# A 4-layer-style hybrid decoder step: the intra-chunk matrix of its gated recurrence built from blocks of four quarters instead of by halving

## The chip, the core and the metric

The kernel runs on one core of one Trainium2 chip. A core has five engines with instruction streams of their own, which meet only at semaphores: TensorE (PE in the profile, its weight loads PEld), VectorE (DVE), ScalarE (ACT), GpSimd (POOL) and SyncE (SP), which here issues the DMAs. SBUF holds working data in 128 partitions, PSUM takes the results of matmuls. The metric is the device time of one execution in microseconds (us), lower is better.

## The reference, cut to what matters

Two layers. Each projects its input, runs sliding-window attention on one part of the columns and a gated linear recurrence (HGRN2) on the other, multiplies both by gates, and maps them to the output. The prompt has 2048 tokens, and 8 samples of 8 tokens each are decoded beside it. The part at issue is the recurrence, four heads of 128 by 128:

```python
G = jnp.cumsum(gc, axis=1)                 # running sum of log forget gates
diff = G[:, :, None] - G[:, None, :]
decay = jnp.exp(jnp.where(causal, diff, NEG_INF))
A = jnp.einsum('bthd,bshd,btshd->bhts', qc, kc, decay)
o = einsum('bhts,bshv->bthv', A, vc) + einsum('bthd,bhdv->bthv', qc * exp(G), S)
S = exp(G_last)[..., None] * S + einsum('bshd,bshv->bhdv', kc * exp(G_last[:, None] - G), vc)
```

A[t, s] is the sum over the 128 key dimensions d of q[t,d] k[s,d] exp(G[t,d] - G[s,d]), for s up to t. The exponent is at most 0. Factors exp(G[t]) and exp(-G[s]) can't be applied apart over a long stretch, since exp(-G[s]) grows without bound, so a kernel picks a token m between s and t and uses exp(G[t]-G[m]) and exp(G[m]-G[s]), both at most 1.

## The kernel before

The kernel is written by hand in phases, each with one instruction stream per engine: constants, and then for each of the two layers attention, recurrence and output. All engines meet at a barrier between phases. The order on an engine is the order in the code, nothing schedules it. Waits are on named semaphores. `wait_apart` puts a wait on a semaphore increment of its own ahead of the instruction.

The recurrence phase walks 17 tiles of 128 tokens, tile 0 being the 64 sample tokens. All tensors of a tile hold heads and tokens in the free dimension (4 x 128 = 512 columns) and key dimensions in the partitions. Its functions are `front` (DVE), `front_log` and `front_exp` (ACT), which turn the projections of a tile into `kT` and the running sum `G`; `middle` on each engine, which builds A; and `output_and_update` on PE. `front` of tile n+1 stands behind `middle` of tile n on DVE.

A is built by seven levels, of half-block lengths 64, 32, 16, 8, 4, 2, 1. A level of length h covers, in each block of 2h tokens, the pairs with t in the second half and s in the first:

- DVE, `sub_level` (L1181, L1182): two subtractions of 256 columns each write the exponents of both halves to E.
- ACT, `middle` (L1046): one exponential of 512 columns on E.
- POOL, `level` (L960): two products, q times E (256 columns, compact in qE) and k times E (256 columns, in kE).
- PE, `level` (L1353): for each of four heads a matmul of kE (128 x 128 weights) with 64 columns of qE, into the PSUM bank LV.
- DVE, `take_level` (L1193): one predicated copy of 256 columns takes from LV what belongs to the level's blocks, with the mask `levels`.

E, qE, kE and LV have two buffers each, used in turn. Last come four matmuls of q and k without decay (`diagonal`, L1360) into the bank M and a copy of the diagonal (L1226, 512 columns). A matmul of float32 data counts as two MATMUL instructions in the trace (8 instructions for the four heads of a level), one of the projections (split into rounded parts, float32r) as one.

PE interleaves this with the projections of the next tile, in `step` (from L1393): q(n+1), levels 0 and 1, transposes of the finished tile's result (L1343), f(n+1), levels 2 and 3, transposes of q and f (L1335, L1337, which need ACT's copy `zqf`, L1011), half of g(n+1), level 4, the other half of g, levels 5 and 6, the diagonal, v(n+1), the transposes of k (L1367), output and state update (L1376 to L1382). Tile 1 and the last tile have levels with no projection between them.

## Time and profile before

| | us |
|---|---|
| median of 3 runs (3099.20 to 3102.58) | 3102.14 |
| profiled execution, its own time | 3102.25 |
| its span, first to last instruction | 3100.6 |
| PE busy | 2827.0 (91%) |
| DVE busy | 1585.9 (51%) |
| POOL busy | 1058.6 (34%) |
| ACT busy | 1026.2 (33%) |

The span runs from the first to the last instruction, and the execution takes 1.65 us more. The shares are means over three kinds of phase. In layer 0 attention ends at about 387 us, the recurrence runs until about 1045 us, and the output phase until about 1540 us; layer 1 follows in the same shape. In a row of a timeline the first number is the start, the second the duration, and in brackets stands how long the engine had been idle and what released it. The duration of an instruction reaches about 0.1 us into the next one where two follow each other freely, so the cost of one in a row of many is the distance between starts. A row with "x8" merges eight instructions that follow one another.

### The profile page before, as it was taken

How to read it: one execution, taken by the hardware profiler on the slowest of the kernel's cores; microseconds unless marked ns; L12 is line 12 of the kernel's file. 1: busy time of each engine (PE TensorE's matmuls, PEld its weight loads, DVE VectorE, ACT ScalarE, POOL GpSimd, SP SyncE). 2: the span in 40 equal slices, each digit the busy share in tenths (PEclk: the TensorE clock that was granted, in tenths of full speed). 3: DMA queues.
4: the chain of work that ended last, by engine and by line, in shares of the span. 5: the costliest groups of instructions: out<-in, count | busy, mean ns of one | idle time of the engine just before them, and what ended most of it. 6: DMA issues, size and time to landing. Idle time of an engine off the chain costs nothing. (4 is left out here: it accounts for less than half of the span.)

```text
span 3100.6 us, 43735 instructions
## 1 busy us (share of the span) xinstructions
PE 2827.0 (91%) x15322; PEld 2373.2 (77%) x15322; DVE 1585.9 (51%) x3037; ACT 1026.2 (33%) x2172; POOL 1058.6 (34%) x940
## 2 busy tenths in 40 slices
PE   6999869999999489999869998699999995899998
PEld 5777658888888478888657776588888884788886
DVE  4666655666766532222246666556666665322222
ACT  3333233444444411111133332334444444111111
POOL 1222122555555323333112221225555553233331
PEclk9999978999999699999889998789999996999999
DMA  4111311000000412222231113110000004122221
GB/s 152 41 41 41 124 38 58 25 21 27 20 24 14 177 58 87 86 86 86 93 111 41 41 41 124 38 58 25 21 27 20 24 14 177 58 87 86 86 81 61
DMA packets 96923, 195.20 MB, mean 63 GB/s; under 512 B 10913, under 2 KB 56225, under 8 KB 94753
## 3 DMA queue, kind: packets, MB, share of 16 engines
q1 hardware_dynamic: 96832, 194.05, 18.6%
q8 instruction: 50, 0.82, 0.1%
q14 instruction: 41, 0.33, 0.0%
HBM read 135.10 MB, written 60.82 MB: 63 GB/s over the span
## 5 line engine op out<-in xcount | busy, mean ns | idle before, releaser
L103 PE MATMUL r_Z<-w_rec_high,w_rec_xh 128*128 128x512 f32 x1088 | 446.4, 410 | 39.2 <-POOL w_rec_xl L951 30.7
L103 PE MATMUL r_Z<-w_rec_high,w_rec_xl 128*128 128x512 f32 x1088 | 430.5, 396 | 0.0
L103 PE MATMUL r_Z<-w_rec_low,w_rec_xh 128*128 128x512 f32 x1088 | 429.6, 395 | 0.0
L103 PE MATMUL a_Z<-w_attn_high,w_attn_xh 128*128 128x512 f32 (+1 forms) x816 | 303.2, 372 | 0.0
L103 PE MATMUL a_Z<-w_attn_low,w_attn_xh 128*128 128x512 f32 (+1 forms) x816 | 291.8, 358 | 0.0
L103 PE MATMUL a_Z<-w_attn_high,w_attn_xl 128*128 128x512 f32 (+1 forms) x816 | 291.0, 357 | 0.0
L1353 PEld LDWEIGHTS r_LV<-r_qE,r_kE 128*128 128x128 f32 x1840 | 249.1, 207 | 51.8 <-POOL r_kE L960 31.0
L960 POOL TENSOR_TENSOR r_qE<-r_qT,r_E 128x256 f32<-128x256 f32 x230 | 191.1, 831 | 281.2 <-ACT r_E L1046 152.3
L1353 PE MATMUL r_LV<-r_qE,r_kE 128*128 128x64 f32 x1840 | 250.4, 290 | 34.9 <-POOL r_kE L960 25.3
L103 PEld LDWEIGHTS r_Z<-w_rec_high,w_rec_xh 128*128 128x128 f32 x1088 | 209.0, 192 | 79.2 <-issue 40.7
L1193 DVE COPY_PREDICATED r_A<-levels,r_LV 128x256 f32<-128x256 int32 x230 | 121.6, 529 | 250.6 <-issue 166.9
L1758 PE MATMUL o_MX<-w_out_high,o_mh 128*128 128x512 f32 x512 | 204.1, 399 | 45.4 <-DVE w_out_low L140 45.4
L103 PEld LDWEIGHTS r_Z<-w_rec_high,w_rec_xl 128*128 128x128 f32 x1088 | 207.7, 191 | 46.5
L103 PEld LDWEIGHTS r_Z<-w_rec_low,w_rec_xh 128*128 128x128 f32 x1088 | 209.2, 192 | 39.3
L1046 ACT ACTIVATE r_E<-r_E 128x512 f32<-128x512 f32 x230 | 145.3, 633 | 265.8 <-DVE r_E L1182 265.8
L1587 POOL TENSOR_TENSOR o_ml<-o_mraw,o_mh 128x1024 fp32r<-128x1024 f32 x34 | 83.6, 2458 | 405.6 <-ACT o_mh L1638 405.6
L1758 PE MATMUL o_GT<-w_out_high,o_hh 128*128 128x512 f32 x544 | 216.1, 397 | 0.0
L960 POOL TENSOR_TENSOR r_kE<-r_kT,r_E 128x256 f32<-128x256 f32 x230 | 213.0, 926 | 0.0
L1758 PE MATMUL o_GT<-w_out_high,o_hl 128*128 128x512 f32 x544 | 212.9, 391 | 0.0
L1758 PE MATMUL o_GT<-w_out_low,o_hh 128*128 128x512 f32 x544 | 212.8, 391 | 0.0
L1758 PE MATMUL o_MX<-w_out_high,o_ml 128*128 128x512 f32 x512 | 201.3, 393 | 0.0
L1758 PE MATMUL o_MX<-w_out_low,o_mh 128*128 128x512 f32 x512 | 200.7, 392 | 0.0
(247 smaller groups left out, 5622.1 us busy)
## 6 DMA issues: line engine op xcount, KB each, us to landing
w_attn_xraw<-dram_xT SPq DMA_DIRECT2D x34, 512.0 KB, 3.4
r_xraw<-dram_xT SPq DMA_DIRECT2D x34, 512.0 KB, 3.3
o_mraw<-dram_mixT SPq DMA_DIRECT2D x34, 512.0 KB, 4.4
dram_y_all<-o_hb SPq DMA_DIRECT2D x34, 512.0 KB, 2.9
dram_xT<-o_yT SPq DMA_DIRECT2D x34, 512.0 KB, 5.2
w_rec_whole<-dram_w_in SPq DMA_DIRECT2D x16, 1024.0 KB, 12.1
w_attn_whole<-dram_w_in SPq DMA_DIRECT2D x16, 640.0 KB, 8.1
dram_mixT<-a_mixT SPq DMA_DIRECT2D x136, 64.0 KB, 2.1
```

The source lines that it names most:

```text
L103: mm = pe.matmul(out, a[:, c, :], b[:, c, :], start=(first and c == chunks[0] and a is xh and b is wh), stop=(last and c == chunks[-1] and ...
L960: op = pool.tensor_tensor(to, halves(flat(q_or_k), h)[half], halves(E[i][:, :], h)[half], ALU.mult)
L1046: act.activation(E[l % 2][:, :], E[l % 2][:, :], ACT.Exp).then_inc(S["level_exp"], 1)
L1193: dve.copy_predicated(to, mask, src).then_inc(S["level_took"], 1)
L1353: mm = pe.matmul(LV[i][:, 64 * g:64 * g + 64], kE[i][:, g * P:(g + 1) * P], qE[i][:, g, :], start=True, stop=True)
L1587: pool.tensor_tensor(ml[:, :, :], mraw[:, :, :], mh[:, :, :].bitcast(F32), ALU.subtract)\
L1758: mm = pe.matmul(out[0][:, out[1]], a[:, c, :], w, start=(c == 0 and a is high and b is wh), stop=(c == chunks - 1 and a is low))
```

## The change

A is now built in three rounds of four-quarter blocks, quarter lengths m = 32, 8, 2, each cut in two units of two heads (`units`, six in a tile), and then one step of neighbouring tokens together with the diagonal.

In a block of 4m tokens with quarters 0 to 3, all six pairs of a later with an earlier quarter are covered at once. The key side has three scaled quarters (each to its own end, 192 columns for two heads, kE). The query side has six slots: quarters 1, 2, 3 scaled from the end of the quarter before them, quarters 2, 3 from two before, and quarter 3 from three before (`LAGS`; 192, 128 and 64 columns for two heads). Per unit:

- DVE, `spans`: four subtractions (192, 192, 128, 64 columns) in place of two of 256.
- ACT: one exponential of 576 columns in place of 512.
- POOL, `scale`: four products (192, 192, 128, 64 columns) in place of two of 256.
- PE, `unit`: two matmuls of 192 columns in place of four of 64.
- DVE, `take`: three predicated copies (192, 128, 64 columns), each behind a wait for the one before, in place of one of 256.

Behind the six units `spans_next` (DVE, 256 columns), an exponential of 256 columns and `scale_next` (POOL, 256 columns) prepare the odd tokens for their left neighbours. `q_next` holds q's 128 tokens and those 64 side by side, so four matmuls of 192 columns (`neighbours`), two into each LV bank, give both the diagonal and the neighbours. `take_next` copies them in four dependent copies (128 and 256 columns, for each pair of heads). The diagonal no longer uses the bank M. Tile 0 takes two units (m = 2) in place of three levels.

The masks of the quarters are made on DVE in the constants phase, from the table that was loaded before, by 19 small instructions, each waited for. DMAs are the same. The sample states' row products now lie in E instead of kE.

On DVE, the end of `middle` in a tile of the loop, with the buffer numbers; r_LV0 and r_LV1 are the PSUM banks, the name in brackets is the semaphore waited for. Before:

```order
L1182 TENSOR_TENSOR r_E0<-r_G 128x256
L1193 COPY_PREDICATED r_A<-levels,r_LV0 128x64x4 [waits level_took,level_mm]
L1220 TENSOR_TENSOR r_kh<-r_G 128x512 [waits khT_ps]
L1193 COPY_PREDICATED r_A<-levels,r_LV1 128x128x2 [waits level_took,level_mm]
L1193 COPY_PREDICATED r_A<-levels,r_LV0 128x256 [waits level_took,level_mm]
L1226 COPY_PREDICATED r_A<-diagonal,r_M 128x512 [waits level_took,diag_ps]
L1139 SCALAR_TENSOR_TENSOR r_lsig<-r_Z,r_expo 128x1024 [waits gate_done,kx_done,act_ln]
```

The same place now:

```order
L1286 TENSOR_TENSOR r_kh<-r_G 128x512 [waits khT_ps]
L1245 COPY_PREDICATED r_A<-quarters,r_LV0 128x32x6 [waits level_mm,level_took]
L1245 COPY_PREDICATED r_A<-quarters,r_LV0 128x32x4 [waits level_took]
L1245 COPY_PREDICATED r_A<-quarters,r_LV0 128x32x2 [waits level_took]
L1245 COPY_PREDICATED r_A<-quarters,r_LV1 128x32x6 [waits level_mm,level_took]
L1245 COPY_PREDICATED r_A<-quarters,r_LV1 128x32x4 [waits level_took]
L1245 COPY_PREDICATED r_A<-quarters,r_LV1 128x32x2 [waits level_took]
L1254 COPY_PREDICATED r_A<-neighbours,r_LV0 128x128 [waits level_mm,level_took]
L1257 COPY_PREDICATED r_A<-diagonal,r_LV0 128x256 [waits level_took]
L1254 COPY_PREDICATED r_A<-neighbours,r_LV1 128x128 [waits level_mm,level_took]
L1257 COPY_PREDICATED r_A<-diagonal,r_LV1 128x256 [waits level_took]
L1176 SCALAR_TENSOR_TENSOR r_lsig<-r_Z,r_expo 128x1024 [waits gate_done,kx_done,act_ln]
```

Three copies behind the key differences have become ten, each waiting for its predecessor, ahead of the first instruction of the next tile's `front`.

On DVE, from the third level to the fifth in the same `middle`, before:

```order
L1182 TENSOR_TENSOR r_E0<-r_G 128x16x16
L1193 COPY_PREDICATED r_A<-levels,r_LV0 128x4x64 [waits level_mm]
L1181 TENSOR_TENSOR r_E1<-r_G 128x32x8 [waits level_prod]
L1182 TENSOR_TENSOR r_E1<-r_G 128x32x8
L1193 COPY_PREDICATED r_A<-levels,r_LV1 128x8x32 [waits level_took,level_mm]
L1181 TENSOR_TENSOR r_E0<-r_G 128x64x4 [waits level_prod]
```

Now, from the third unit to the fifth:

```order
L1224 TENSOR_TENSOR r_E0<-r_G 128x8x8
L1245 COPY_PREDICATED r_A<-quarters,r_LV0 128x2x96 [waits level_mm,level_took]
L1245 COPY_PREDICATED r_A<-quarters,r_LV0 128x2x64 [waits level_took]
L1245 COPY_PREDICATED r_A<-quarters,r_LV0 128x2x32 [waits level_took]
L1219 TENSOR_TENSOR r_E1<-r_G 128x192 [waits level_prod]
L1224 TENSOR_TENSOR r_E1<-r_G 128x8x24
L1224 TENSOR_TENSOR r_E1<-r_G 128x8x16
L1224 TENSOR_TENSOR r_E1<-r_G 128x8x8
L1245 COPY_PREDICATED r_A<-quarters,r_LV1 128x2x96 [waits level_mm,level_took]
L1245 COPY_PREDICATED r_A<-quarters,r_LV1 128x2x64 [waits level_took]
L1245 COPY_PREDICATED r_A<-quarters,r_LV1 128x2x32 [waits level_took]
L1219 TENSOR_TENSOR r_E0<-r_G 128x192 [waits level_prod]
```

Between the third and the fifth unit's exponents stand six copies where there were two.

On PE, behind the second half of the projection g, before:

```order
L1353 MATMUL r_LV1<-r_qE1,r_kE1 128x64 [waits level_took,level_prod]
L1353 MATMUL r_LV1<-r_qE1,r_kE1 128x64 x3
L1353 MATMUL r_LV0<-r_qE0,r_kE0 128x64 [waits level_took,level_prod]
L1353 MATMUL r_LV0<-r_qE0,r_kE0 128x64 x3
L1360 MATMUL r_M<-r_qT,r_kT 128x128 [waits uT_out]
L1360 MATMUL r_M<-r_qT,r_kT 128x128 x3
```

Now:

```order
L1417 MATMUL r_LV1<-r_qE1,r_kE1 128x192 [waits level_took,level_prod]
L1417 MATMUL r_LV1<-r_qE1,r_kE1 128x192
L1426 MATMUL r_LV0<-r_q_next,r_kT 128x192 [waits level_took,level_prod]
L1426 MATMUL r_LV0<-r_q_next,r_kT 128x192
L1426 MATMUL r_LV1<-r_q_next,r_kT 128x192 [waits level_took]
L1426 MATMUL r_LV1<-r_q_next,r_kT 128x192
```

The last pair writes bank LV1, which the unit three rows up has just filled and which DVE must have copied first. The diff, cut to its core:

```diff
+QUARTERS = (32, 8, 2)
-        E = [sb(f"E{i}", [P, GW]) for i in range(2)]
+        q_next, kT, G = sb("q_next", [P, GH, P + P // 2]), ...
+        E = [sb(f"E{i}", [P, 576]) for i in range(2)]
+        units = [(m, half) for m in QUARTERS for half in range(2)]
+        LAGS = ((slice(0, 3), 1), (slice(3, 5), 2), (slice(5, 6), 3))
...
+                def scale(n, u, m, half):
+                    i, at = u % 2, passed(n) + u
+                    pool.wait_ge(S["level_exp"], at + 1)
+                    wait(pool, S["level_mm"], made(n) + max(u - 1, 0))
+                    pool.tensor_tensor(blocks(kE[i][:, :, :], m)[:, :, 0:3, :], ..., ALU.mult)
+                    for at_slot, quarter in LAGS:
+                        of = slice(at_slot.start * m, at_slot.stop * m)
+                        op = pool.tensor_tensor(to[:, :, :, of], q[:, :, :, quarter * m:], decays[:, :, :, of], ALU.mult)
+                    op.then_inc(S["level_prod"], 1)
...
+                def take(n, u, m, half):
+                    wait_apart(dve, S["dve_passed"], S["level_mm"], made(n) + u + 1)
...
+                    for i, (at_slot, quarter) in enumerate(LAGS):
...
+                            wait_apart(dve, S["dve_passed"], S["level_took"], taken(n) + 3 * u + i)
+                        dve.copy_predicated(rows[:, :, :, quarter * m:], ..., src[:, :, :, of]).then_inc(S["level_took"], 1)
...
                 def middle(n, k, units):
                     dve.wait_ge(S["sum_done"], n + 1)
-                    for l, h in enumerate(levels):
-                        sub_level(n, l, h)
+                    for u, (m, half) in enumerate(units):
+                        spans(n, u, m, half)
...
-                        if l >= 2:
-                            take_level(n, l - 2, levels[l - 2])
+                        if u >= 2:
+                            take(n, u - 2, *units[u - 2])
+                    spans_next(n, len(units))
...
+                    for u in (len(units) - 2, len(units) - 1):
+                        take(n, u, *units[u])
+                    for half in range(2):
+                        take_next(n, len(units) + half, half)
...
+                def unit(n, u):
+                    pe.wait_ge(S["level_prod"], passed(n) + u + 1)
+                    wait(pe, S["level_took"], taken(n) + 3 * max(u - 1, 0))
+                    for g in range(2):
+                        mm = pe.matmul(LV[i][:, 192 * g:192 * g + 192], kE[i][:, g, :], qE[i][:, g, :], start=True, stop=True)
+                    mm.then_inc(S["level_mm"], 1)
...
+                def neighbours(n, u):
+                    pe.wait_ge(S["level_prod"], passed(n) + u + 1)
+                    for half in range(2):
+                        pe.wait_ge(S["level_took"], taken(n) + 3 * (u - 1 + half))
+                        for g in range(2):
+                            mm = pe.matmul(LV[half][:, 192 * g:192 * g + 192], kT[:, 2 * half + g, :],
+                                           q_next[:, 2 * half + g, :], start=True, stop=True)
+                        mm.then_inc(S["level_mm"], 1)
```

## Rows read from the trace of the kernel before

**Rows 1.** Busy time in a stretch: us, PE, PEld, DVE, ACT, POOL, PEclk, DMA share, GB/s

```profile
650.00:700.00 50.00, 50.00 (x302) 44.10 (x301) 30.60 (x62) 23.80 (x44) 28.55 (x31) 1.00 0.06 21
```

**Rows 2.** Timeline of PE, tiles of the loop, layer 0: start, duration, instruction

```profile
707.04 1.06 PE L1382 MATMUL r_M<-r_v,r_khT 128*128 128x128 f32 x8
707.86 0.48 PE L103 MATMUL r_Z<-w_rec_high,w_rec_xh 128*128 128x512 f32 x1
...
730.27 1.89 PE L1353 MATMUL r_LV<-r_qE,r_kE 128*128 128x64 f32 x16
...
747.00 2.04 PE L1353 MATMUL r_LV<-r_qE,r_kE 128*128 128x64 f32 x16
748.88 0.60 PE L1343 MATMUL r_M<-ident,r_u 128*128 128x128 f32 x4
754.80 1.89 PE L1353 MATMUL r_LV<-r_qE,r_kE 128*128 128x64 f32 x16
756.53 0.61 PE L1335 MATMUL r_Z<-ident,r_zqf 128*128 128x128 f32 x4
...
763.85 1.89 PE L1353 MATMUL r_LV<-r_qE,r_kE 128*128 128x64 f32 x16
```

**Rows 3.** Timeline of DVE, the same tile

```profile
732.39 0.75 DVE L1193 COPY_PREDICATED r_A<-levels,r_LV 128x256 f32<-128x256 int32 x1 [0.23 <-PE r_LV L1353]
733.31 0.75 DVE L1226 COPY_PREDICATED r_A<-diagonal,r_M 128x512 f32<-128x512 int32 x1 [0.17 <-DVE r_A L1193]
733.95 1.21 DVE L1139 SCALAR_TENSOR_TENSOR r_lsig<-r_Z,r_expo 128x1024 f32<-128x1024 f32 x1
...
749.03 0.44 DVE L1193 COPY_PREDICATED r_A<-levels,r_LV 128x256 f32<-128x256 int32 x1
749.36 0.42 DVE L1181 TENSOR_TENSOR r_E<-r_G 128x256 f32<-128x256 f32 x1
...
752.29 0.94 DVE L1182 TENSOR_TENSOR r_E<-r_G 128x256 f32<-128x256 f32 x1
```

**Rows 4.** Timeline of POOL, the same tile

```profile
732.98 2.41 POOL L951 TENSOR_TENSOR w_rec_xl<-r_xraw,w_rec_xh 128x1024 fp32r<-128x1024 f32 x1
...
744.69 0.74 POOL L960 TENSOR_TENSOR r_qE<-r_qT,r_E 128x256 f32<-128x256 f32 x1 [0.29 <-ACT r_E L1046]
745.39 0.93 POOL L960 TENSOR_TENSOR r_kE<-r_kT,r_E 128x256 f32<-128x256 f32 x1
```

**Rows 5.** Timeline of ACT, the same tile

```profile
753.27 0.63 ACT L1046 ACTIVATE r_E<-r_E 128x512 f32<-128x512 f32 x1 [2.01 <-DVE r_E L1182]
755.00 1.02 ACT L1011 ACTIVATE r_zqf<-r_Z 128x1024 f32<-128x1024 f32 x1 [1.09 <-PE r_Z L103]
```

**Rows 6.** Timeline of DVE, diagonals of tiles 1, 15 and 16, layer 0

```profile
531.51 0.75 DVE L1226 COPY_PREDICATED r_A<-diagonal,r_M 128x512 f32<-128x512 int32 x1 [0.18 <-PE r_M L1360]
...
1002.90 0.74 DVE L1226 COPY_PREDICATED r_A<-diagonal,r_M 128x512 f32<-128x512 int32 x1 [0.18 <-PE r_M L1360]
...
1033.26 0.72 DVE L1226 COPY_PREDICATED r_A<-diagonal,r_M 128x512 f32<-128x512 int32 x1 [1.08 <-PE r_M L1360]
```

**Rows 7.** Timeline of DVE in the constants phase

```profile
9.58 0.17 DVE L1890 TENSOR_SCALAR c_bounds<-c_lb 128x4 f32<-128x4 f32 x1
9.79 0.17 DVE L1891 TENSOR_SCALAR c_bounds<-c_rest 128x4 f32<-128x4 f32 x1
```

**Rows 8.** Timeline of PE: idle before its matmuls, in brackets

```profile
42.63 0.74 PE L676 MATMUL a_SC<-ident,a_qk 128*128 128x128 f32 x5 [2.86 <-POOL a_qk L293]
...
1016.00 3.79 PE L1353 MATMUL r_LV<-r_qE,r_kE 128*128 128x64 f32 x16 [4.65 <-POOL r_kE L960]
```

**Rows 9.** Busy time in three more stretches, columns as in the first group

```profile
15.00:20.00 5.00, 0.00 (x0) 0.00 (x0) 1.49 (x1) 0.18 (x1) 0.00 (x0) 1.00 1.02 396
40.00:45.00 5.00, 2.37 (x21) 2.40 (x21) 1.46 (x4) 3.40 (x7) 1.55 (x2) 1.00 0.03 7
1000.00:1050.00 50.00, 33.67 (x177) 30.62 (x175) 28.58 (x59) 17.77 (x41) 20.09 (x22) 0.68 0.56 210
```

More of the change, by code:

```diff
@@ L1113, in after @@
                             copy_z(n + 1)
-                    middle(n, LEVELS, after)
+                    middle(n, units, after)
                     front_log(n + 1)
@@ L1196, in middle @@
+                def middle(n, k, units):
                     dve.wait_ge(S["sum_done"], n + 1)
-                    for l, h in enumerate(levels):
-                        sub_level(n, l, h)
-                        if l == 0:
+                    for u, (m, half) in enumerate(units):
+                        spans(n, u, m, half)
+                        if u == 0:
                             silu(n, k)
-                        if l == 1 and isinstance(n, int) and n == 1:
+                        if u == 1 and isinstance(n, int) and n == 1:
@@ L1435, in _ @@
                 project(1, 1, "q")
-                level(0, 0, DEC_LEVELS[0])
-                level(0, 1, DEC_LEVELS[1])
-                level(0, 2, DEC_LEVELS[2])
-                diagonal(0)
+                unit(0, 0)
+                unit(0, 1)
+                neighbours(0, 2)
                 project(1, 1, "f")
@@ L1460, in _ @@
                 t.then_inc(S["o_done"], 1)
-                level(1, 0, LEVELS[0])
-                level(1, 1, LEVELS[1])
-                for l in (2, 3):
-                    level(1, l, LEVELS[l])
+                for i in range(4):
+                    unit(1, i)
                 transpose_u(0)
@@ L1467, in _ @@
                 project(2, 0, "g", 0, KC // 2)
-                level(1, 4, LEVELS[4])
+                unit(1, 4)
                 project(2, 0, "g", KC // 2, KC)
-                for l in (5, 6):
-                    level(1, l, LEVELS[l])
-                diagonal(1)
+                unit(1, 5)
+                neighbours(1, NU)
                 project(2, 0, "v")
@@ L1482, in _ @@
                 step(n - 1, 1)
-                level(n, 0, LEVELS[0])
-                level(n, 1, LEVELS[1])
+                unit(n, 0)
+                unit(n, 1)
                 transpose_u(n - 1)
-                for l in range(2, NL):
-                    level(n, l, LEVELS[l])
-                diagonal(n)
+                for i in range(2, NU):
+                    unit(n, i)
+                neighbours(n, NU)
                 transpose_kh(n)
```

215 lines of the change are left out of this document (123 added, 92 removed).

## The prediction

> **What bounds the kernel now.** I read the busy time by stretch first, then PE's timeline of one tile, and then DVE, POOL and ACT beside it. In a stretch inside the recurrence PE is busy for all of its 50.00 us at full clock, while DVE has 30.60 and POOL 28.55 [rows 1]. So PE sets the pace, and the change takes work from PE. But PE's queue is full only because the others hand over just in time. The timelines show how little room there is. One turn of the loop can be cut in three legs, all from the end of the projection g. A: from PE at 730.27 to the first instruction of DVE's `front` at 733.95, 3.68 us. B: from there to PE's first level at 747.00, 13.05 us. C: from there over levels 0 to 4, f and g to the next 763.85, 16.85 us. That makes 33.58 us [rows 2, 3]; the diagonals of tiles 1 and 15, 14 turns apart, give 33.67 [rows 6]. In leg B POOL has level 0's products ready at 745.39 + 0.93 = 746.32, 0.68 us before PE wants them [rows 2, 4]. In leg C ACT waits only 1.09 us for PE before it copies q and f [rows 5]. These are the cushions, and they are small.
>
> **What PE gains.** Levels 0 and 1 cost 748.88 - 747.00 = 1.88 us, two later ones 756.53 - 754.80 = 1.73, so eight matmuls of 64 columns cost 0.22 to 0.235 each; eight instructions (four matmuls) of 128 columns cost 707.86 - 707.04 = 0.82, or 0.205 each [rows 2]. Between 64 and 128 columns nothing grows. A tile has 28 matmuls for its levels and four for the diagonal, 1.88 + 1.73 + 0.8 + 1.73 + 0.82 = 7.0 us. The new one has 16 of 192 columns, a width that no row shows. Flat growth gives 0.205, twice the 128-column one 0.41; growth with the columns gives 1.5 x 0.21 = 0.32, which I take as nearest to that row. 16 x 0.32 = 5.1 us, so PE has 1.9 us less work in a tile (3.7 to 0.4). If PE stayed the bound, that would be the gain.
>
> **What the others pay.** DVE: free copies of 256 columns start 0.33 apart (749.03 to 749.36), one of 512 columns holds the next back by 733.95 - 733.31 = 0.64. So a copy costs about 0.02 plus 0.0012 per column. A copy that waits for the one before starts 0.17 behind its visible end (732.39 + 0.75 to 733.31), where a free one starts 0.1 ahead of it: 0.27 for each dependence [rows 3]. A `take` is then 3 x 0.02 + 384 x 0.0012 + 2 x 0.27 = 1.1 us in place of 0.33. The bounds of a dependence are 0 (a free neighbour) and 0.27; small instructions of the constants phase that wait without an increment between them start 0.21 apart at 0.17 duration [rows 7], in between. I take 0.27, since it is the same kind of copy with the same kind of wait.
>
> The Trainium skill says otherwise (VectorE: DVE Perf Modes, The DRAIN you can't avoid): a semaphore behind every copy costs nothing, eight copies took the same with and without. By it a take would cost 0.5 and not 1.1. Here the row of the diagonal copy speaks against it; what the rule would make of the time is a rival below.
>
> POOL: products of 256 columns start 745.39 - 744.69 = 0.70 apart, one of 1024 takes 2.41 [rows 4], so about 0.16 plus 0.0021 per column. A unit is 4 x 0.16 + 576 x 0.0021 = 1.85 us in place of 1.40; beside DVE level 0 took 1.63, so I count 2.1. A tile has six and one of 0.7, about 12 to 13 us as before: POOL's total isn't the matter, the delay of the first unit is. DVE's subtractions are the contended work: 0.42 alone, 0.94 while POOL works (752.29, POOL being in its products of the next levels) [rows 3]. ACT has 0.06 more per unit.
>
> **The sum, leg by leg.** A: unit 5 (0.64) and PE's hand-over (0.3), then seven dependent copies: three of unit 5, four of `take_next`. Their 1152 columns cost 7 x 0.02 + 1.38 = 1.5, short runs in A 0.3 (the copy at 732.39, whose runs are one element, takes 0.75 where 749.03 takes 0.44), six dependences 1.6, the last visible end nothing. 4.4 us, 0.7 more than now. ACT's logarithm, on which `front` also waits, was just in time for 733.95 and isn't later. Queued behind these copies is all of `front`, and behind that ACT, POOL and PE's next unit.
>
> B: `front` is unchanged. The exponents of unit 0 cost 0.1 more, the exponential 0.06, POOL 0.5; the cushion of 0.68 gives back 0.55 (PE starts some 0.1 behind a release). 13.15 us.
>
> C: five units in place of five levels save 1.88 + 1.73 + 0.8 - 5 x 0.64 = 1.2 us. Unit 1 must wait, because its products come 2.1 us behind those of unit 0 and PE needs 0.64 for unit 0: 1.5 us. The transposes of q and f need ACT's copy, which stands behind the exponential of unit 4, and that behind DVE's exponents, now with two dependent takes ahead (1.6 more), longer subtractions beside POOL (0.8 more) and a start 0.6 nearer to PE. Of these 3.0 the old idle of 1.09 and PE's own lateness (1.5 - 0.6) cover 2.0. PE waits 1.0. C is 16.85 - 1.2 + 1.5 + 1.0 = 18.15, with 0.1 for unit 3 that comes late too 18.25.
>
> 35.8 us in place of 33.6, 2.2 to 2.3 more; 28 such turns in two layers, 2.3 x 28 = 64 us. A further stall of PE, before the second pair of `neighbours` (it waits for three copies of unit 5, some 1.1 us), lies beside legs A and B. PE's own work fills them before, 3.68 + 13.05 = 16.7 us; less the old levels 5 and 6 and the diagonal (1.73 + 0.82), plus 3 x 0.64 and 1.1, it is 17.2 of the 17.5 that A and B now take. So the stall costs nothing as long as they are late.
>
> Outside the loop: tile 1 has four units in a row without a projection, each paced by POOL and DVE, about +2. The last tile takes 1033.26 - 1002.90 = 30.4 us [rows 6] and DVE is idle little there; six takes and the last four copies add 5.5 us of DVE, of which idle takes 2 to 3: +3. Both for two layers, +10. Tile 0 has three small steps in place of three levels and a diagonal, and a projection behind them: 0. The masks are 19 instructions of 0.2 us [rows 7], 3.8 us before the first phase. The DMA engines are full with weights until 20 us [rows 9], and what attention needs first queues behind these: I count 1.5 of 3.8. The profiled execution took 3102.25, the median is 3102.14, so nothing is to be scaled: 3102 + 64 + 10 + 1.5 = 3178.
>
> **Rivals.** *PE stays the bound.* DVE is idle 39% of the stretch, and if the copies fall into that idle time, the handovers cost nothing. The price is 28 x -1.9 = -53, with 8 for ends and start: 3057. It decides once the waits of all legs sum to less than PE's 1.9; I count 4.2. For it speaks only the share of DVE; against it, that its idle time lies where it waits for PE, and the copies where it is waited for. 0.13 for all of this side above 0.2%.
>
> *Dependences are nearly free.* Leg A loses 1.6, leg C 0.5: 33.7 us a turn, 28 x 0.1 = 3, ends 8: 3113. This is also where the skill's rule leads. Against it the 0.17 gap, which every diagonal of the loop shows. 0.10.
>
> *The clock falls.* PE would be idle twice within a few us, about 0.6 before unit 0 and 1.5 before unit 1. After an idle of 4.65 us (at 1016.00) a pair of levels takes 3.79 in place of 2.04, and the granted clock of that stretch is 0.68, partly its 1.2 GHz level; after one of 2.86 it stays 1.00, at 2.4 GHz [rows 2, 8, 9]. A fall in each turn would cost about as much as it lasts, over half of it: with 4 to 5 us at half clock 2.2 us a turn, 3178 + 62 = 3240. 0.10.
>
> *No measurable change*, mechanisms between the first two: 0.05. The forecast itself 0.62.
>
> **How the numbers follow.** 3178 is the likeliest. Its own range comes from the dependence (0.1 less each is 0.6 in leg A and 0.1 in C: -20), the width of the matmul (flat: -10, doubled: +12), and the four-part instructions (0.1 more fixed on DVE and POOL each: +1.5 a turn, +40): 3145 to 3225. The free dependence and the clock belong inside as well: 3112 to 3240, with about 2 in 10 outside. 0.2%, about 6 us, is what a measurement here tells from no change. Faster 0.13, same 0.05, slower 0.82.
>
> **What would show it.** PE is no longer busy through a stretch in the recurrence: idle before unit 0 and unit 1, before the transposes of q and f, before the second half of `neighbours`, 4 us a tile. Diagonals 35.8 us apart in the loop. Copies of a take 0.17 behind each other. `front` on DVE starts 4.4 behind the end of g. I am wrong if PE stays full, if takes cost near 0.5 us, or if PEclk falls in the loop.

## The result, and the profile after

The changed kernel takes 3164.22 us (median of 4 runs, 3162.18 to 3167.4), the kernel before beside it 3101.73: a ratio of 1.0204, 95% interval 1.0186 to 1.0221. The profiled execution has a span of 3163.8 us. 3178 was forecast: the direction and the likeliest case came out, and the forecast was 14 us too high.

Busy time of a stretch, of one turn of the loop and of a piece in it (us, PE, PEld, DVE, ACT, POOL, PEclk, DMA share, GB/s):

```profile
650.00:700.00 50.00, 45.04 (x230) 37.44 (x229) 40.22 (x107) 22.01 (x39) 30.20 (x50) 1.00 0.06 21
675.67:711.30 35.63, 32.64 (x170) 27.38 (x169) 27.88 (x75) 16.28 (x31) 19.89 (x30) 1.00 0.07 22
727.00:730.40 3.40, 3.40 (x12) 2.93 (x11) 3.10 (x10) 0.79 (x2) 2.12 (x4) 0.50 0.00 0
```

PE is no longer full: 45.04 of 50.00 us in place of 50.00, while DVE rose from 30.60 to 40.22 [rows 1]. The third row is one of seven stretches of 3.4 us in the 28 turns in which PE ran at half clock.

Timeline of PE in that turn. The numbers and the brackets read as in the rows of the kernel before:

```profile
688.48 0.92 PE L1417 MATMUL r_LV<-r_qE,r_kE 128*128 128x192 f32 x4
691.06 0.92 PE L1417 MATMUL r_LV<-r_qE,r_kE 128*128 128x192 f32 x4 [1.66 <-POOL r_qE L986]
...
699.44 0.66 PE L1399 MATMUL r_Z<-ident,r_zqf 128*128 128x128 f32 x4 [0.27 <-ACT r_zqf L1047]
...
706.57 0.81 PE L1417 MATMUL r_LV<-r_qE,r_kE 128*128 128x192 f32 x4
707.22 0.81 PE L1426 MATMUL r_LV<-r_q_next,r_kT 128*128 128x192 f32 x4
709.09 0.92 PE L1426 MATMUL r_LV<-r_q_next,r_kT 128*128 128x192 f32 x4 [1.06 <-DVE r_A L1245]
```

PE idles 1.66 us before unit 1, 0.27 before the transposes of q and f and 1.06 before the second half of the neighbours, 3.0 us in all; before unit 0, where the prediction had an idle too, none is recorded.

Timeline of DVE, the same turn, from `front` to the next `front`:

```profile
675.67 1.22 DVE L1176 SCALAR_TENSOR_TENSOR r_lsig<-r_Z,r_expo 128x1024 f32<-128x1024 f32 x1
...
682.29 0.69 DVE L1199 TENSOR_TENSOR r_lsig<-r_expo 128x512 f32<-128x512 f32 x1 [1.36 <-ACT r_expo L1073]
...
691.48 0.36 DVE L1245 COPY_PREDICATED r_A<-quarters,r_LV 128x192 f32<-128x192 int32 x1
691.99 0.68 DVE L1245 COPY_PREDICATED r_A<-quarters,r_LV 128x128 f32<-128x128 int32 x2 [0.15 <-DVE r_A L1245]
...
694.58 1.19 DVE L1245 COPY_PREDICATED r_A<-quarters,r_LV 128x192 f32<-128x192 int32 x3
695.68 0.68 DVE L1219 TENSOR_TENSOR r_E<-r_G 128x192 f32<-128x192 f32 x1
696.28 1.48 DVE L1224 TENSOR_TENSOR r_E<-r_G 128x192 f32<-128x192 f32 x3
...
707.71 1.32 DVE L1245 COPY_PREDICATED r_A<-quarters,r_LV 128x192 f32<-128x192 int32 x3 [2.16 <-PE r_LV L1417]
709.18 0.45 DVE L1254 COPY_PREDICATED r_A<-neighbours,r_LV 128x128 f32<-128x128 int32 x1
709.77 0.45 DVE L1257 COPY_PREDICATED r_A<-diagonal,r_LV 128x256 f32<-128x256 int32 x1
710.37 0.45 DVE L1254 COPY_PREDICATED r_A<-neighbours,r_LV 128x128 f32<-128x128 int32 x1
710.96 0.45 DVE L1257 COPY_PREDICATED r_A<-diagonal,r_LV 128x256 f32<-128x256 int32 x1
711.30 1.22 DVE L1176 SCALAR_TENSOR_TENSOR r_lsig<-r_Z,r_expo 128x1024 f32<-128x1024 f32 x1
```

Timelines of POOL (unit 0) and ACT (exponential of unit 4, copy of q and f, logarithm):

```profile
686.41 0.72 POOL L979 TENSOR_TENSOR r_kE<-r_kT,r_E 128x192 f32<-128x192 f32 x1 [0.62 <-ACT r_E L1083]
687.09 1.34 POOL L986 TENSOR_TENSOR r_qE<-r_q_next,r_E 128x192 f32<-128x192 f32 x3
```

```profile
697.79 0.68 ACT L1083 ACTIVATE r_E<-r_E 128x576 f32<-128x576 f32 x1 [1.93 <-DVE r_E L1224]
698.38 1.00 ACT L1047 ACTIVATE r_zqf<-r_Z 128x1024 f32<-128x1024 f32 x1
...
708.91 1.06 ACT L1063 ACTIVATE r_expo<-r_expo 128x1024 f32<-128x1024 f32 x1
```

The legs read as in the prediction: A, 706.57 to 711.30, is 4.73 us; B, 675.67 to 688.48, 12.81; C, 688.48 to 706.57, 18.09: a turn of 35.63. The last diagonals of tiles 1, 15 and 16 give the rest:

```profile
532.08 0.45 DVE L1257 COPY_PREDICATED r_A<-diagonal,r_LV 128x256 f32<-128x256 int32 x1
...
1034.79 0.44 DVE L1257 COPY_PREDICATED r_A<-diagonal,r_LV 128x256 f32<-128x256 int32 x1
...
1068.78 0.44 DVE L1257 COPY_PREDICATED r_A<-diagonal,r_LV 128x256 f32<-128x256 int32 x1
```

502.71 us for 14 turns where 471.39 stood [rows 6]: +31.3, and +28.4 in the other layer, 59.7 of the 62.5 us. The last tile takes 33.99 in place of 30.36, +3.6, in layer 0, and 33.35 in place of 30.38, +3.0, in layer 1.

### The profile page after: what moved, and what is told of

Its sections match the earlier page's. It is cut to its first block and busy times, and to the rows that moved or that the text cites. A ratio compares the mean times of both kernels' runs of the same rounds, so it can differ in the third digit from the quotient of the medians.

```text
span 3163.8 us, 44242 instructions
## 1 busy us (share of the span) xinstructions
PE 2790.0 (88%) x14266; PEld 2294.5 (73%) x14266; DVE 1754.0 (55%) x3874; ACT 1032.9 (33%) x2172; POOL 1111.3 (35%) x1298
## 5 line engine op out<-in xcount | busy, mean ns | idle before, releaser
L986 POOL TENSOR_TENSOR r_qE<-r_q_next,r_E 128x192 f32<-128x192 f32 (+2 forms) x588 | 315.9, 563 | 0.0
L1245 DVE COPY_PREDICATED r_A<-quarters,r_LV 128x192 f32<-128x192 int32 (+2 forms) x588 | 186.0, 316 | 184.8 <-PE r_LV L1417 126.9
L1083 ACT ACTIVATE r_E<-r_E 128x576 f32<-128x576 f32 (+1 forms) x230 | 148.2, 645 | 376.6 <-DVE r_E L1224 344.0
L1417 PE MATMUL r_LV<-r_qE,r_kE 128*128 128x192 f32 x784 | 182.7, 366 | 96.1 <-POOL r_qE L986 83.7
L1417 PEld LDWEIGHTS r_LV<-r_qE,r_kE 128*128 128x128 f32 x784 | 143.5, 207 | 132.9 <-POOL r_qE L986 107.5
L1224 DVE TENSOR_TENSOR r_E<-r_G 128x192 f32<-128x192 f32 (+2 forms) x588 | 221.8, 429 | 0.0
L1790 DVE SCALAR_TENSOR_TENSOR o_th<-o_th,o_PL 128x1024 f32<-128x1024 f32 x34 | 41.5, 1221 | 311.8 <-PE o_PL L1822 311.8
L979 POOL TENSOR_TENSOR r_kE<-r_kT,r_E 128x192 f32<-128x192 f32 x196 | 119.1, 608 | 240.0 <-ACT r_E L1083 199.6
```

The costliest lines, as they stand in the source:

```text
L979: pool.tensor_tensor(blocks(kE[i][:, :, :], m)[:, :, 0:3, :], blocks(kT[:, pair(half), :], m)[:, :, 0:3, :], E[i][:, 0:192].rearrange("p ( ...
L986: op = pool.tensor_tensor(to[:, :, :, of], q[:, :, :, quarter * m:], decays[:, :, :, of], ALU.mult)
L1083: act.activation(decays, decays, ACT.Exp).then_inc(S["level_exp"], 1)
L1224: op = dve.tensor_tensor(to[:, :, at_slot, :], g[:, :, quarter:, :], ends[:, :, 0:many, :].to_broadcast([P, nb, many, m]), ALU.subtract)
L1245: dve.copy_predicated(rows[:, :, :, quarter * m:], mask[:, :, of].unsqueeze(1).to_broadcast([P, 2, nb, many]), src[:, :, :, of]).then_inc( ...
L1417: mm = pe.matmul(LV[i][:, 192 * g:192 * g + 192], kE[i][:, g, :], qE[i][:, g, :], start=True, stop=True)
```

## The experiments

Ratios are to the kernel before, run on the same chip (medians 3100.9 to 3103.0), with 95% intervals. "Idle" is PE's in one turn.

**1. The dependences between copies.** Copies 2 and 3 of a take, and the diagonals, go to tensors of their own, so that their waits reach further back. A isn't gathered.

```diff
+                        to = s_dec[1 + i] if apart and i else A
-                            wait_apart(dve, S["dve_passed"], S["level_took"], taken(n) + 3 * u + i)
+                            wait_apart(dve, S["dve_passed"], S["level_took"], taken(n) + 3 * u + i - (2 if apart else 0))
```

> The changed kernel with its three copies per unit kept, each of the same size, but the second and third (and the copies of the diagonal) written to tensors of their own from tile 2 on, so that no copy waits for its neighbour; A lacks their part. If it is the waits between the copies that make the last leg (end of g to front) long, front starts when ACT's logarithm is ready, 1.3 us earlier in a turn (711.30 to 709.97 in the changed kernel's trace), and the copies in the middle give some 0.3 more: 1.6 x 28 = 45, 3119 us. If it is the number of copies or their own time on DVE, nothing changes: 3164. If dependences were free anyway, also 3164.

Measured: 3122.86 us, 1.0065 (1.0048 to 1.0082), 41 less than the changed kernel. A turn takes 34.45, and none has a half-clock stretch. Leg A is 3.86 (0.87 less), B 12.99 (0.18 more), C 17.60 (0.49 less): 1.2 a turn where I expected 1.6. Copies that don't wait for each other (DVE's timeline):

```profile
688.16 0.37 DVE L1250 COPY_PREDICATED r_A<-quarters,r_LV 128x192 f32<-128x192 int32 x1
688.43 0.42 DVE L1250 COPY_PREDICATED r_s_dec<-quarters,r_LV 128x128 f32<-128x128 int32 x2
```

0.27 us from one start to the next, where the changed kernel has 691.99 - 691.48 = 0.51. The increments are still there; only the wait for the copy just issued is gone. So the waits cost 28 x 1.17 = 33 us, and with them went the 8 us of half clock. The Trainium skill (VectorE: DVE Perf Modes, The DRAIN you can't avoid) says that a semaphore behind every copy costs nothing extra. This trace agrees for the increment (0.27 with it), and not for a wait on the copy just ahead (0.51).

**2. POOL's products.** Two of the three products of q in a unit are left out.

```diff
-                    for at_slot, quarter in LAGS:
+                    for at_slot, quarter in LAGS[:1]:
```

> The changed kernel with one of three query products per unit on POOL (two of four products left out, the result lacks them). If the first two units reach PE late because POOL takes 2.0 us for each, unit 0 comes 0.8 and unit 1 1.2 us earlier, and less contention with DVE gives a little more: 1.2 to 1.4 us a turn, 3125 to 3130 us. If only DVE's copies count, POOL's products are hidden: 3160 or more. If PE were the bound, 3164.

Measured: 3115.23 us, 1.0044 (1.0029 to 1.006); a turn of 34.44, 1.18 less, and PE waits 0.69 for unit 1. The 49 us are these turns (33), the 8 us of half clock and some 8 us in tile 1 and the last tile, which I hadn't counted. The number is near the expected one, but the reason that I gave isn't the one in the trace. DVE's three subtractions beside POOL take 1.09 us in place of 1.48, so that units 2, 3 and 4 take 0.4 us less each, and DVE is done with unit 4's exponents 20.92 us behind `front` (687.35 + 1.09 - 667.52) in place of 22.09 (696.28 + 1.48 - 675.67): 1.17 less, the whole gain of the turn. POOL's products cost time by slowing DVE, and not by coming late to PE (experiment 6). DVE's timeline of this kernel:

```profile
667.52 1.22 DVE L1176 SCALAR_TENSOR_TENSOR r_lsig<-r_Z,r_expo 128x1024 f32<-128x1024 f32 x1
...
687.35 1.09 DVE L1224 TENSOR_TENSOR r_E<-r_G 128x192 f32<-128x192 f32 x3
```

**3. PE's width.** The new matmuls take 128 columns from tile 2 on.

```diff
+                        width = 192 if isinstance(n, int) and n < 2 else 128
-                        ... qE[i][:, g, :], start=True, stop=True)
+                        ... qE[i][:, g, 0:width], start=True, stop=True)
```

> The changed kernel with matmuls of 128 instead of 192 columns from tile 2 on (a third of the columns left out). PE then has 16 x 0.11 = 1.75 us less work in a tile. If PE's work is no longer the bound, only the units between the waits count (unit 1, unit 4, unit 5, about 0.5 us a turn): 3149 us. If the wider matmul is what costs, 28 x 1.75 = 49: 3115 us.

Measured: 3160.61 us, 1.0182 (1.0165 to 1.0199), neither number. Undisturbed turns take 35.17, 0.45 less, about the 0.5 expected, but nearly every second one (12 of 28) takes 36.1, with 3.4 us at half clock. PE's waits grow to 0.35, 1.78, 0.85 and 1.26. PE isn't the bound: with less work it idles more, and in this kernel its clock falls more often.

**4. The kernel before, with each level's copy cut in three dependent ones.**

```diff
-                    dve.copy_predicated(to, mask, src).then_inc(S["level_took"], 1)
+                    for i, of in enumerate((slice(0, 2), slice(2, 3), slice(3, 4))):
+                        if i:
+                            wait_apart(dve, S["dve_passed"], S["part_took"], 2 * (passed(n) + l) + i)
+                        dve.copy_predicated(to[:, of], mask[:, of], src[:, of])...
```

> The kernel before with one part of the change alone: each level's copy of 256 columns cut in three (two heads, one, one), each waiting for the one before. The two copies behind the last levels get 0.58 us longer each and are still taken in turn, so front starts about 0.9 later; the cushion before level 0 (0.55 us) takes most: +0.4 us a turn, 3113 us (3106 to 3122). If dependences between copies are free, or DVE's 39% idle time takes them: 3102 us.

Measured: 3137.84 us, 1.0112 (1.0093 to 1.013), 16 us above my range. Leg A fits (PE's level 5, then DVE's timeline):

```profile
702.61 1.89 PE L1357 MATMUL r_LV<-r_qE,r_kE 128*128 128x64 f32 x16
```

```profile
703.75 1.34 DVE L1196 COPY_PREDICATED r_A<-levels,r_LV 128x128 f32<-128x128 int32 x3 [2.00 <-PE r_LV L1357]
705.33 1.34 DVE L1196 COPY_PREDICATED r_A<-levels,r_LV 128x128 f32<-128x128 int32 x3 [0.23 <-DVE r_A L1196]
706.84 0.75 DVE L1230 COPY_PREDICATED r_A<-diagonal,r_M 128x512 f32<-128x512 int32 x1 [0.17 <-DVE r_A L1196]
```

1.51 to 1.58 us from copy to copy in place of 0.92 (732.39 to 733.31) to 0.98 [rows 3]. Leg A, from PE's 702.61 to `front` at 707.48, is 4.87 in place of 3.68: 1.19 more, which is 4 dependences of 0.27 and a little. What I had left out is leg C (17.38, with 0.38 idle before level 1), tile 1 and the last tile, about 3 and 2 longer in a layer, and two half-clock stretches. So dependent copies alone, without the rest of the change, can slow the loop: 36 us. That isn't a share of the change's 62.5, since this kernel has 14 more copies and 14 dependences in a tile and none of PE's gain.

**5. The last copies in DVE's wait for ACT.**

```diff
                     dve.tensor_tensor(expo[:, 0, :], ..., ALU.subtract).then_inc(S["gap_done"], 1)
+                    if not first(n) and not (isinstance(n, int) and n == 1):
+                        take_late(n - 1)
```

> The changed kernel, with the four copies of `take_next` moved on DVE from leg A to the place where DVE waits 1.36 us for ACT's logarithm, behind the subtraction `gap` of the next tile's `front` (order: both neighbours, then both diagonals, so that each waits two back). If only the legs count, leg A ends with ACT's logarithm, some 3.5 us behind g in place of 4.73, leg B grows by 0.3, a turn takes 34.6 and the kernel 3136 us. My theory also counts who needs A: PE's output matmuls now start 9.2 us behind the end of g, and A is finished only 3.5 + 5.3 + 0.2 + 1.7 = 10.7 us behind it. PE waits 1.5 us there, and since PE had only 0.3 us to spare before unit 0, that unit comes 1.1 us later than now: a turn of 36.7, 3195 us. That would say that DVE's idle time isn't free to use, because of when its result is wanted.

Measured: 3154.57 us, 1.0166 (1.0149 to 1.0183). Turns of 35.4 to 35.5 and no half clock; my 3195 was wrong, and so was 3136, the number if only the legs count. A is 3.4 as expected, but B 14.9. PE does wait for A, 0.66, yet that isn't what counts. ACT and DVE of this kernel:

```profile
643.92 0.60 ACT L1102 ACTIVATE r_khT<-r_M 128x512 f32<-128x512 f32 x1 [5.33 <-PE r_M L1452]
644.41 0.62 ACT L1071 ACTIVATE r_expo<-r_expo 128x512 f32<-128x512 f32 x1
```

```profile
642.52 0.69 DVE L1197 TENSOR_TENSOR r_expo<-r_expo 128x512 f32<-128x512 f32 x1
643.13 0.72 DVE L1303 COPY_PREDICATED r_A<-neighbours,r_LV 128x128 f32<-128x128 int32 x2
643.72 0.77 DVE L1308 COPY_PREDICATED r_A<-diagonal,r_LV 128x256 f32<-128x256 int32 x2
645.73 0.69 DVE L1201 TENSOR_TENSOR r_lsig<-r_expo 128x512 f32<-128x512 f32 x1 [1.24 <-ACT r_expo L1073]
```

`gap` is ready at 643.2, but ACT's exponential starts at 644.41, behind the copy of khT, which waits for PE's transposes, and these don't come earlier. What leg A gives, ACT's order takes.

**6. Unit 1 later on PE.**

```diff
                     unit(n, 0)
+                    project(n + 1, 1 - k, "f", 0, KC // 2)
+                    transpose_u(n - 1)
                     unit(n, 1)
-                    project(n + 1, 1 - k, "f")
+                    project(n + 1, 1 - k, "f", KC // 2, KC)
```

> The changed kernel, with PE's order alone changed: unit 1 stands behind half of the projection f and the transposes of u, and no longer right behind unit 0. My theory says that PE's wait for unit 1 (1.66 us) lies on the path: leg C shrinks by 1.5 us, a turn takes 34.1 in place of 35.6, the half-clock stretches go, 3164 - 28 x 1.5 - 8 = 3114 us. Rival: DVE, ACT and POOL pace leg C, and the wait only moves to the transposes of q and f and to units 2 and 3; then leg C stays near 17.8 and the time near 3150.

Measured: 3181.5 us, 1.0249 (1.0232 to 1.0266). An undisturbed turn takes 35.6 as in the changed kernel, 12 turns take 37.2 with half clock. My theory (3114) fell. The rival was right on leg C, 17.95, but its 3150 leaves out the clock. PE waits elsewhere, and ACT starts unit 4's exponential at the same time as ever:

```profile
665.13 0.91 PE L1417 MATMUL r_LV<-r_qE,r_kE 128*128 128x192 f32 x4 [1.07 <-POOL r_qE L986]
666.77 0.66 PE L1399 MATMUL r_Z<-ident,r_zqf 128*128 128x128 f32 x4 [0.72 <-ACT r_zqf L1047]
```

```profile
665.12 0.68 ACT L1083 ACTIVATE r_E<-r_E 128x576 f32<-128x576 f32 x1 [1.91 <-DVE r_E L1224]
665.71 1.01 ACT L1047 ACTIVATE r_zqf<-r_Z 128x1024 f32<-128x1024 f32 x1
```

665.12 is 22.09 us behind this tile's `front` (643.03); in the changed kernel it is 697.79 - 675.67 = 22.12, with narrower matmuls 22.09, before 753.27 - 733.95 = 19.32 [rows 3, 5]. DVE, ACT and POOL get there by themselves in these three kernels, whatever PE does, and DVE has no idle but 0.15 us per dependence from 8.9 us behind `front` on. Behind that point ACT copies q and f, and from the transposes on PE has 7.1 us of work without a wait (699.44 to 706.57). That sets leg C.

**7. The second half of the neighbours later on PE.**

```diff
-                    neighbours(n, NU)
-                    project(n + 1, 1 - k, "v")
+                    neighbours(n, NU, (0,))
+                    project(n + 1, 1 - k, "v", 0, 2)
+                    neighbours(n, NU, (1,))
+                    project(n + 1, 1 - k, "v", 2, KC)
```

> The changed kernel, with the second half of the neighbours moved on PE behind the first two chunks of the projection v, where the copies that it waits for are done. My theory (the prediction's) says that this wait of 1.06 us costs nothing while PE waits for unit 0 anyway: PE idles 1.3 us before unit 0 instead of 0.3, the copies of the neighbours come 0.5 us later at most, and the time stays at 3158 to 3172. Rival: the wait is on the path, as is each other wait of PE, and its 1.06 us come back 28 times: 3135 us.

Measured: 3181.05 us, 1.0255 (1.0238 to 1.0272). The stall costs nothing, as predicted: an undisturbed turn is 35.62 with and without. But the time missed 3158 to 3172 and went up, because 17 turns of 36.8 stand where there were seven. PE's waits now follow each other, and the clock halves at 694.0, 0.7 us behind the second of them:

```profile
690.69 0.92 PE L1417 MATMUL r_LV<-r_qE,r_kE 128*128 128x192 f32 x4 [1.33 <-POOL r_qE L986]
693.27 1.02 PE L1417 MATMUL r_LV<-r_qE,r_kE 128*128 128x192 f32 x4 [1.66 <-POOL r_qE L986]
```

**8. Four moves at once.** Half of experiment 5, with 6 and 7, and two chunks of q ahead of the output.

```diff
+                        take_next(n - 1, NU + 1, 1)
...
+                    project(n + 2, k, "q", 0, 2)
                     transpose_kh(n)
                     output_and_update(n)
```

> The changed kernel, with four moves in the order of the work and nothing else. DVE's copies of the second half of the neighbours go behind `gap` of the next tile (1.2 us into a wait of 1.36), those of the first half stay. PE: unit 1 behind half of f, the second half of the neighbours behind two chunks of v, and the first two chunks of the next q before the output matmuls, so that these needn't wait for the late copies; the output of heads 0 and 1 waits for their copies only. If the legs are as I describe them, A is 3.55 in place of 4.73, B 12.9, C 16.6 in place of 18.09, a turn of 33.1, and there are no half-clock stretches: 3164 - 28 x 2.5 - 8 = 3086 us, below the kernel before. Rival: the path goes on through ACT and POOL, which pace leg C (17.3) and, with the squares later on ACT, leg B (13.6): a turn of 34.4, 3120 us.

Measured: 3165.2 us, 1.0206 (1.0186 to 1.0225). A 3.57 as expected, B 13.9, C 18.0, turns of 35.5 and seven half-clock stretches. The rival was right that ACT and POOL carry the path on, as in 5 and 6, but its 3120 was 45 us too low: it had C at 17.3.

**9. Interleaved copies, and the order of all engines.** First the three copies of a take between the next subtractions:

```diff
-                        spans(n, u, m, half)
-                            take(n, u - 2, *units[u - 2])
+                        spans(n, u, m, half, copies(n, u - 2, *units[u - 2]) if u >= 2 else ())
```

> The changed kernel, in which the three dependent copies of each take stand between the four subtractions of the next unit's exponents on DVE (subtraction, copy, subtraction, copy, ...) and no longer in a row; the copies of unit 5 alternate in the same way with those of the neighbours of the other two heads. Same instructions, same waits, another order. Theory formed from the runs so far: DVE is busy without a gap from `front` to the exponents of unit 4 and paces leg C, and PE's waits are its shadow. Then the waits of a copy for the one before fall away where DVE paces: three takes x 2 x 0.27 us = 1.6 us, less what the later handover of the exponents costs; a turn of 34.4, no half-clock stretches, 3164 - 28 x 1.2 - 8 = 3122 us (3112 to 3132). Rival: leg C is paced by the round over ACT and POOL (exponential 0.7, products 2.2), which an interleaved take makes 1 us longer for each unit; then 3175 us or more.

The edit does more than "same waits": each of the three copies now has the wait for PE of its own, with an increment, which had stood ahead of the first alone. That makes 12 more of them in a tile.

Measured: 3294.48 us, 1.062 (1.0602 to 1.0637), turns of 38.5 to 43.3, with 22 falls of the clock. It lies in the rival's range (3175 or more), but not for the rival's reason. DVE's timeline:

```profile
662.54 0.36 DVE L1221 TENSOR_TENSOR r_E<-r_G 128x192 f32<-128x192 f32 x1 [2.00 <-issue]
...
678.47 0.37 DVE L1253 COPY_PREDICATED r_A<-quarters,r_LV 128x192 f32<-128x192 int32 x1 [4.89 <-PE r_LV L1432]
```

The copy of unit 2 waits for PE, where unit 2 stands behind f, and the rest of unit 4's exponents now stand behind that copy. And just behind the loop's branch, in every second turn (the loop's body holds two tiles), DVE issues nothing for 2.0 us; the last section has what the trace shows of it.

Then, with all work kept, the order of four engines:

```diff
-                            new_state(n - 1)
-                            gated(n - 1, 1 - k)
...
+                    if late:
+                        new_state(n - 1)
+                    for copy in copies(n, len(units) - 2, *units[-2]):
+                        copy()
+                    if late:
+                        gated(n - 1, 1 - k)
```

> As the kernel with interleaved copies, and the rest of the work ordered by what the runs showed. DVE: the new state and the gated output of the tile before (2.5 us) go from between the exponents of units 1 and 2 to its idle time at the end of leg C; the last copies of the neighbours go behind `gap`. ACT: the squares and the copy of v stand behind the exponential of unit 0, the copy of q and f one unit earlier, the copy of the transposed output behind the logarithm. POOL: the root of the tile before stands behind unit 2. PE: unit 1 behind three chunks of f, the second half of the neighbours and the transposes of u behind two chunks of v, the first two chunks of q behind the transposes of kh. All work is kept. If DVE paces legs B and C and PE has 32.3 us of work in a turn, this takes 2.5 us from DVE's path and 1.2 from leg A: A 3.5, B 12.9, C 16.2, a turn of 32.6, 3164 - 28 x 3.0 - 8 = 3072 us (3060 to 3095), below both kernels. Rival: a round that I don't see (ACT and POOL in leg C) holds the turn at 34 or more: 3112 us or more.

Measured: 3144.11 us, 1.0128 (1.0111 to 1.0145), the rival's side (3112 or more); turns of 33.5 and 35.5 alternate, with the wait for PE and the stall behind the branch as before. Taken back in the next kernel, together with the 12 extra waits of a tile, which the expectation doesn't name:

```diff
-                        spans(n, u, m, half, copies(n, u - 2, *units[u - 2]) if u >= 2 else ())
+                        spans(n, u, m, half)
+                            for copy in copies(n, u - 2, *units[u - 2]):
+                                copy()
...
-                    wait_apart(dve, S["dve_passed"], S["level_mm"], made(n) + u + 1)
+                    if only == 0:
+                        wait_apart(dve, S["dve_passed"], S["level_mm"], made(n) + u + 1)
```

> The kernel of the last run (v9_order) with one thing taken back: the copies of units 0 to 3 stand in a row behind the next unit's exponents again, as in the changed kernel, and not between the subtractions. Its trace showed two causes for its 3144 us. In every turn DVE's first copy of a take, now in front of the other three subtractions, waited for PE (0.6, 1.1 and 2.2 us for units 0, 1 and 2), where unit 2 stands behind all of f, and held back the exponents of unit 4 with it. In every second turn DVE issued nothing for 1.9 us behind the loop's branch, which no kernel with the takes in a row shows. Theory: the rest of the order is good, and with both gone the turns that took 33.5 take 32.6 (A 3.45, B 13.3, C 15.8), all alike: 3144 - 14 x 0.9 - 14 x 3.0 = about 3090 us or somewhat less (3070 to 3100), below the kernel before. Rival: DVE without the interleaving pays 1.6 us of dependences in leg C again, turns of 33.6 and more without the branch's stall: 3110 to 3125 us.

Measured: 3127.05 us, 1.0078 (1.0064 to 1.0092), turns of 33.6 to 34.0: 2 us above the rival's range, and the stall behind the branch is gone. The trace has DVE waiting 1.25 for ACT (the copy of khT again) and up to 1.75 for POOL, and PE 0.7 to 1.0 before unit 3. The two things taken back aren't told apart by this run.

```diff
                     front_log(n + 1)
+                    gap_log(n + 1)
                     copy_khT(n)
...
+                    unit(n, 2)
+                    project(n + 1, 1 - k, "g", 0, 1)
                     transpose_qf(n + 1)
+                    unit(n, 3)
```

> The kernel of the last run (v10_order2) with what its trace still showed idle taken out, by order alone. ACT: exponential and logarithm behind `gap` come before the copy of khT (DVE waits 1.25 us there, of which 0.8 is that copy). DVE: the new state goes back behind the exponents of unit 1, where DVE now waits 1.75 us for POOL. POOL: the root stands behind unit 3, since PE waited 0.96 us for unit 3's products. PE: one chunk of g and the transposes of q and f stand in front of unit 3, and the second half of the neighbours behind three chunks of v. Theory: legs A 3.5, B 13.1, C 15.9, a turn of 32.5 in place of 33.85: 3127 - 28 x 1.3 = 3090 us (3080 to 3102), below both kernels. Rival: DVE's own work, 30.5 us of a turn with hardly a wait left where it matters, holds the turn at 33.3 or more: 3112 us or more.

Measured: 3074.59 us, 0.9911 (0.9894 to 0.9927): 5 us below my range, and the only kernel below the one before, by 27 us. One turn, and the wait of DVE that was 1.36:

```profile
665.47:697.40 31.93, 31.93 (x170) 27.29 (x169) 29.36 (x75) 16.32 (x31) 20.21 (x31) 1.00 0.07 25
```

```profile
672.09 0.69 DVE L1221 TENSOR_TENSOR r_lsig<-r_expo 128x512 f32<-128x512 f32 x1 [0.40 <-ACT r_expo L1076]
```

PE is busy for the whole turn of 31.93 us, 1.65 less than before, close to the 1.9 that the prediction gave PE. 28 turns give 49 us (they took 33.73 in the mean before, here 31.98). Some 23 of them are lost again: 11 in the first, second and last tiles, for which this order wasn't made, 9 between the last tile of a layer and the next layer or the end, and 2.5 ahead of the first `front`, whose start differs by 3 us between kernels with the same constants phase (430.1 to 433.4). The kernel before wasn't reordered for comparison. In its loop PE has no idle that another order could take (50.00 of 50.00 [rows 1]); at the ends of its phases it has, so how much of the 27 us is the change's own stays open.

## Why the prediction was right, and where it wasn't

**The mechanism held**: PE gains less on its matmuls than the hand-overs cost. Of the steps, in its own terms:

- PE's gain. Two matmuls of 192 columns start 707.22 - 706.57 = 0.65 ahead of the next, 0.325 each, as taken. The 1.9 us less of work in a turn is 1.65 where PE is never idle (experiment 9).
- A take: 695.68 - 694.58 = 1.10, predicted 1.1. A dependence costs 0.24 in experiment 1 (0.51 - 0.27) and 0.27 by my rows.
- Leg A 4.73, predicted 4.4. `front` stands 1.3 behind ACT's logarithm (708.91 + 1.06 = 709.97), so these copies are what it waits for. The four of `take_next` start 0.59 to 0.60 apart and cost 2.1. I had counted the whole leg 0.3 short: the first copy starts 1.14 behind PE's unit 5 (707.71 - 706.57), counted 0.94, and the seven copies take 3.59 (to 711.30), counted 3.4.
- Leg B 12.81, predicted 13.15. POOL's unit 0 took 2.02, predicted 2.1, and is ready 12.76 behind `front`, before 12.37 [rows 3, 4]: 0.39 later where I had counted 0.66.
- Leg C 18.09, predicted 18.25, the right number from a wrong sum, which is luck. I added a wait for unit 1 (1.5, measured 1.66) and one for q and f (1.0, measured 0.27), and with these as measured the sum gives 17.7. The missing 0.4 is the units themselves: beside a wait they hold PE for 0.92 (unit 0) and 0.75 (unit 1) and not 0.64. The wait for q and f came out short because of a cushion that I had overlooked: before, ACT's copy ended at 755.00 + 1.02 = 756.02, 0.51 ahead of PE's transposes at 756.53 [rows 2, 5]. Nor are the two waits separate terms: experiment 6 removes the first and gets 1.07 and 0.72 instead. The true term is DVE's way to unit 4's exponents. Counted from `front` it is 2.8 us longer than before (22.12 to 19.32), counted from PE's unit 0 3.04 (9.31 to 6.27). I had that as 3.0 in a side sentence; it should have been the leg.
- The second half of the neighbours: stall 1.06, predicted 1.1, costing nothing in an undisturbed turn (experiment 7).
- Ends: the last tile +3.6 and +3.0, predicted +3. Tile 1's diagonals end at 532.53 and ended at 532.26; from the first `front` of the layer that is +0.8, and +0.4 in layer 1, predicted +2. The masks, predicted 1.5: nothing that can be seen, the first `front` starts at 430.13 and started at 430.64. The output phases take back 3.9 of what the loops bring. Outside the 28 turns 2.8 us are left of the 11.5 forecast: this is most of the 14 us.
- The range: flat, doubled and the four-part instructions, -10, +12 and +40, add up to 3230 at the top and not to 3225. It changes nothing here.

The turns, forecast at 64, make 59.7: an undisturbed one takes 35.6 where the mean was 33.73 (33.67 and 33.78 in the two layers), 28 x 1.87 = 52, and seven half-clock stretches of 1.2 make 8. These 8 us aren't in the sum of the forecast; without them the turns would have been 12 us below it, so a part of the nearness is luck. PEclk falling in the loop was named as a sign of being wrong, and the clock rival did come true in a quarter of the turns, at 1.2 us and 3.4 us at half clock where it had 2.2 and 4 to 5; no run shows a stretch of 4 to 5 by itself. "PE stays the bound" was rightly unlikely for this order of the work; in experiment 9, with every queue ordered anew, PE is the bound again. "Dependences are nearly free" fell with experiment 1.

The loss isn't split into independent shares: without the dependences a turn is 1.17 shorter, with two products less on POOL 1.18, and both shorten the same path, DVE's way to unit 4, where they need not add up.

## What to carry to other kernels

An engine's waits in a trace may be the shadow of another's full queue: move one away, and if the turn keeps its length, look for the engine whose instructions reach a fixed point at the same distance in both runs. In-order queues make position a cost of its own: the same work took 3164 and 3075 us, and a copy that has to wait, put in front of work that doesn't, held the queue for far longer than it takes itself (4.89 us for a copy of 0.37 on DVE in experiment 9; on ACT the copy of khT in experiment 5). A change that trades one long instruction for dependent short ones should be priced with the waits (about 0.25 us each here) on the engine where nothing can be put between them.

## What was not expected of the hardware

- The clock. In the loop it fell to 0.50, the 1.2 GHz level, for 3.4 us at a time (three times for 6.8 in experiment 9), and outside experiment 9 each fall cost a turn 1.0 to 1.9. With PE's idle time in a turn in brackets, the falls in 28 turns are: changed kernel (3.0) 7, experiment 3 (4.2) 12, experiment 6 (2.9) 12, experiment 7 (3.0 to 3.3) 17, experiment 8 (3.1) 7, experiment 4 (0.4 to 0.8) 2, the first two kernels of experiment 9 (5.6 to 7.7 and 1.2 to 3.5) 22 and 1, experiment 5 (2.9), experiments 1 and 2 (2.1) and the last two kernels none. The sum of idle time alone doesn't sort them. Before the fall at 727.0 PE had idled 1.58 ahead of unit 1, before that of experiment 7 1.33 and 1.66 with one unit between, before one of experiment 4 0.17 and 0.63. But other turns with the same waits have no fall, as the one from 640.07 in the changed kernel, also with 1.58, and the one from 605.47 in experiment 7, with 1.33 and 1.66. What decides stays open.
- DVE's 2.0 us without an issue behind the loop's branch, in two of the kernels of experiment 9. Their traces show what goes with it: instructions are fetched again and again. The page's third section lists the DMA queues with packets, MB and share, first the kernel with interleaved copies, then the changed one:

```profile
q14 instruction: 102, 0.84, 0.1%
q14 instruction: 52, 0.43, 0.0%
```

Every other kernel has 41 to 55 packets in this queue, the second with the stall 104. From 660 to 980 us, in the loop, the two with the stall fetch 20 and 21 packets, the changed kernel and the one with the takes put back none, and one of 8 KB starts at 660.54, as the stall does. The trace has 313 and 315 DVE instructions, waits included, from one branch of the loop to the next in these two, and 289 to 291 in all other kernels with the new blocks. The extra waits are 24 of them. So the longer body of the loop, and not the order of the copies, is the likely cause. It isn't shown, since no run has the interleaving without the extra waits.
